# A four-layer decoder trunk: the retention gate's sample sum moved ahead of the norm's scale chain, and the first loads put in another order

## The reference

```python
def rmsnorm(x, g):
    x32 = x.astype(F32)
    return x32 * lax.rsqrt(jnp.mean(x32 * x32, axis=-1, keepdims=True) + EPS) * g

# even layer: one input projection, window attention [A] and spatial gating [B], SiLU gates, output projection
# odd layer (retention):
def odd_layer_prompt(x, g_mix, w_in, w_out):                 # the sample group: the same with a carried state
    q, k, v, g = split_ret(rmsnorm(x, g_mix) @ w_in, bsz, seq)   # 8 heads, keys 256 wide, values 512 wide
    state, o = lax.scan(step, state0, chunks(q, k, v))       # inner + cross per chunk of 128
    return ret_output(x, o, g, w_out), state

def ret_output(x, o, g, w_out):
    on = standardize(o).reshape(bsz, t, R_V_WIDTH)           # per head: (o - mean) * rsqrt(var + EPS)
    return x + (jax.nn.silu(g) * on) @ w_out

def memory_kv(mem, g_mem, w_k, w_v):                         # 256 memory tokens, once for each layer
    h = rmsnorm(mem, g_mem)
    return h @ w_k, h @ w_v
# every layer: cross attention into the memory (4 heads); at the end a last rmsnorm
```

## Time and profile before

| what | us |
|---|---|
| median of three runs | 3490.93 |
| the profiled execution's own time | 3490.97 |
| its span in the trace | 3489.2 |
| PE busy with matmuls | 3290.9 (94%) |
| GpSimd busy | 1052.2 (30%) |
| ACT busy | 998.0 (29%) |
| DVE busy | 916.1 (26%) |
| granted PE clock, mean of the span | 0.979 |

### The profile page before, as it was taken

How to read it: one execution, slowest core, us unless ns; L and a number is a source line. 1 busy time by engine, 2 the same in 40 slices (tenths; PEclk the granted TensorE clock), 3 DMA queues, 4 the chain that set the end, 5 groups by cost and what they waited for, 6 DMA issues and landing times.

```text
span 3489.2 us, 41826 instructions
## 1 busy us (share of the span) xinstructions
PE 3290.9 (94%) x15122; PEld 2567.9 (74%) x15122; DVE 916.1 (26%) x1684; ACT 998.0 (29%) x1526; POOL 1052.2 (30%) x444
## 2 busy tenths in 40 slices
PE   7999999999997999999999999999999989999976
PEld 5887777777886786776768677676867768878865
DVE  2202343332033413222130322214132240120335
ACT  5523333233233421312212131221212221222332
POOL 5632322332331232322313222231322223333311
PEclk9999999999999999999999999999999999999998
DMA  6432222223232243333333333333333344322332
GB/s 241 142 85 89 62 68 61 73 66 119 79 103 81 96 148 121 119 103 102 110 116 118 118 117 100 104 110 121 114 119 106 125 140 140 119 92 79 103 98 84
DMA packets 211053, 374.22 MB, mean 107 GB/s; under 512 B 20449, under 2 KB 59329, under 8 KB 207617
## 3 DMA queue, kind: packets, MB, share of 16 engines
q1 hardware_dynamic: 137744, 233.34, 21.5%
q10 hardware_dynamic: 73152, 138.60, 11.8%
HBM read 312.71 MB, written 60.16 MB: 107 GB/s over the span
## 4 chain that ended last, share of the span: by engine, by line
PE 75%; DVE 5%; ACT 2%; issue 1%; DVEq 1%; DMA 1%; ACTq 0%
PE bank L606 18%; PE bank L608 17%; PE bank L607 17%; PE bank L610 5%; PE bank L611 4%; PE bank L622 3%; PE bank L1032 2%; PE bank L1023 2%; PE bank L1071 1%; PE bank L1067 1%; PE bank L1063 1%; DVE R L1994 1%; DVEq L1782 1%; DVE R L2235 1%; PE bank L928 1%
## 5 line engine op out<-in xcount | busy, mean ns | idle before, releaser
L583 POOL TENSOR_TENSOR w_lo<-w_raw,w_hi 128x1024 fp32r<-128x1024 f32 x440 | 1052.0, 2391 | 2391.7 <-ACT w_hi L1138 2391.2
L606 PE MATMUL bank<-w_hi,xT_hi 128*128 128x512 f32 (+1 forms) x2880 | 1172.9, 407 | 6.5 <-ACT R L1150 2.7
L608 PE MATMUL bank<-w_hi,xT_lo 128*128 128x512 f32 (+1 forms) x2880 | 1125.2, 391 | 0.0
L607 PE MATMUL bank<-w_lo,xT_hi 128*128 128x512 f32 (+1 forms) x2880 | 1123.5, 390 | 0.0
L1138 ACT ACTIVATE w_hi<-w_raw 128x1024 fp32r<-128x1024 f32 x440 | 466.2, 1059 | 1537.6 <-PE bank L611 1437.8
L606 PEld LDWEIGHTS bank<-w_hi,xT_hi 128*128 128x128 f32 x2880 | 546.2, 190 | 144.3 <-issue 34.1
L608 PEld LDWEIGHTS bank<-w_hi,xT_lo 128*128 128x128 f32 x2880 | 544.6, 189 | 116.2
L607 PEld LDWEIGHTS bank<-w_lo,xT_hi 128*128 128x128 f32 x2880 | 546.0, 190 | 114.1 <-issue 11.5
L610 PE MATMUL bank<-w_hi,xT_sample 128*128 128x512 f32 (+1 forms) x816 | 333.4, 409 | 59.8 <-DVE R L1868 59.1
L611 PE MATMUL bank<-w_lo,xT_sample 128*128 128x512 f32 (+1 forms) x816 | 320.8, 394 | 0.0
L622 PE MATMUL bank<-cst,R 128*128 128x128 f32 (+3 forms) x1274 | 192.9, 277 | 61.5 <-DMA R<-in_norm_mem 13.5
(11 more groups left out here) (180 smaller groups left out, 2095.2 us busy)
## 6 DMA issues: line engine op xcount, KB each, us to landing
w_raw<-in_w_in_ret SPq DMA_DIRECT2D x128, 512.0 KB, 3.7
w_raw<-in_w_in_even SPq DMA_DIRECT2D x80, 512.0 KB, 3.6
w_raw<-in_w_in_ret SPq DMA_DIRECT2D x128, 256.0 KB, 2.9
R<-in_state_ret ACTq DMA_DIRECT2D x64, 512.0 KB, 4.4
out_ret_state_sample<-R ACTq DMA_DIRECT2D x64, 512.0 KB, 3.0
w_raw<-in_w_out_ret SPq DMA_DIRECT2D x64, 512.0 KB, 3.7
w_raw<-in_w_out_even SPq DMA_DIRECT2D x32, 512.0 KB, 3.7
mix_scratch<-R ACTq DMA_DIRECT2D x16, 576.0 KB, 3.4
```

What stands on the lines that cost most here:

```text
L583: pool.tensor_tensor(wlo[:, s], raw[:, s], whi[:, s].bitcast(F32), ALU.subtract).then_inc(lo_ready, 1)
L606: pe.matmul(acc, th[:, k, tok], hi[:, kk, 0:width], start=first, stop=False)
L607: pe.matmul(acc, th[:, k, tok], lo[:, kk, 0:width], start=False, stop=False)
L608: mm = pe.matmul(acc, tl[:, k, tok], hi[:, kk, 0:width], start=False, stop=last)
```

## The change

Two edits. In every retention head, DVE now does the gate's `sample_sum` right behind the variances (new function `group_vars`) and ahead of the wait for the root; it waits there for the end of product C (`w_used`). `gate_mul` is called with no counter for it and leaves the sum out. In the even layer `gate_mul` is as before.

At the start, the factors of the memory's two norms come in one load ahead of the memory tokens, the other four rows in two loads behind them, transposed apart at the end of the first product. The x loads move to the third group of the first product. ACT does `hi` of one weight group before it copies the factors, and the other three one by one between the first three halves of the transposed memory tokens.

```diff
-GAINS = ["norm_mix0", "norm_mix1", "norm_cross0", "norm_cross1", "norm_mem0", "norm_mem1"]
+GAINS = ["norm_mem0", "norm_mem1", "norm_mix0", "norm_mix1", "norm_cross0", "norm_cross1"]
+GM = 2 * KT
+GX = 4 * KT
...
-            tp(bank_of("mem", "gains")[:, 0:KT * len(GAINS)], grow[0:KT * len(GAINS), :], KT * len(GAINS)).then_inc(FULL("mem", "gains"), 1)
+            tp(bank_of("mem", "gains")[:, 0:GM], grow, GM).then_inc(FULL("mem", "gains"), 1)
...
+                elif ch == 0 and g == GPC - 1:
+                    pe.wait_ge(xgains_in, 32)
+                    pe.wait_ge(*is_free("mem", "xgains"))
+                    tp(bank_of("mem", "xgains")[:, 0:GX], xgrow, GX).then_inc(FULL("mem", "xgains"), 1)
...
             act.dma_start(cst[:, :], consts).then_inc(consts_in, 16)
+            act.dma_start(grow, I.norm_mem.rearrange("l (k p) -> (l k) p", p=P)).then_inc(gains_in, 16)
             for m in range(2):
                 act.dma_start(memX[:, m], I.mem_prompt[0, m * P:(m + 1) * P, :]).then_inc(mem_in, 16)
-            gains = [I.norm_mix[0], I.norm_mix[1], I.norm_cross[0], I.norm_cross[1], I.norm_mem[0], I.norm_mem[1]]
-            for n, g in enumerate(gains):
-                act.dma_start(grow[KT * n:KT * (n + 1), :], g.rearrange("(k p) -> k p", p=P)).then_inc(gains_in, 16)
-            load_x(False)
-            for s in range(RING):
-                hi(Lin(0), s)
+            for n, g in enumerate((I.norm_mix, I.norm_cross)):
+                act.dma_start(xgrow[GM * n:GM * (n + 1), :], g.rearrange("l (k p) -> (l k) p", p=P)).then_inc(xgains_in, 16)
+            hi(Lin(0), 0)
             act.wait_ge(*is_full("mem", "gains"))
...
             for n in range(3):
                 hi_half("mem", n, n, 0, "norm_mem0")
+                hi(Lin(0), n + 1)
...
+                    if g == 2:
+                        load_x(False)
...
-                v.wait_ge(w_used, L.at(GPC))
-                sample_sum(sbuf[0:NS, :], bank[NT], FREE(stage, (tag, NT)))
+                if L is not None:
+                    v.wait_ge(w_used, L.at(GPC))
+                    sample_sum(sbuf[0:NS, :], bank[NT], FREE(stage, (tag, NT)))
...
                 group_stats(NT)
+                group_vars(h)
+                v.wait_ge(w_used, Lin(L.c + GPC, L.k, L.i).at(GPC))
+                sample_sum(sgs[0:NS, :], bank[NT], FREE(stage, ("C", NT)))
                 group_norm(h)
-                gate_mul(stage, "C", i, 2 + h, Lin(L.c + GPC, L.k, L.i), lambda t: ON[0:rows(t), t], sg, sgs, NT)
+                gate_mul(stage, "C", i, 2 + h, None, lambda t: ON[0:rows(t), t], sg, sgs, NT)
```

More of the change, by code:

```diff
@@ L232, in make_plan @@
     weights("mem", 4)
-    plan.add("mem", [("gains", 5, True)])
+    plan.add("mem", [("gains", 5, True), ("xgains", 4, True)])
     state.xt = 1
@@ L369, in build @@
         gbc = c.take(D)
-        grow = gbc[:, 0:P]
+        grow, xgrow = gbc[0:GM, 0:P], gbc[0:GX, P:2 * P]
         junk = R2[:, 5 * D + 5 * CW:5 * D + 6 * CW]
@@ L432, in build @@
         rstd_ready, xt_hi_ready, stat_zero = sem("rstd_ready"), sem("xt_hi_ready"), sem("stat_zero")
-        gains_in, split_done = sem("gains_in"), sem("split_done")
+        gains_in, xgains_in, split_done = sem("gains_in"), sem("xgains_in"), sem("split_done")
         outs_done, x_saved = sem("outs_done"), sem("x_saved")
@@ L681, in _ @@
             pe.wait_ge(consts_in, 16)
-            pe.wait_ge(gains_in, 16 * len(GAINS))
+            pe.wait_ge(gains_in, 16)
             pe.wait_ge(*is_free("mem", "gains"))
-            tp(bank_of("mem", "gains")[:, 0:KT * len(GAINS)], grow[0:KT * len(GAINS), :], KT * len(GAINS)).then_inc(FULL("mem", "gains"), 1)
+            tp(bank_of("mem", "gains")[:, 0:GM], grow, GM).then_inc(FULL("mem", "gains"), 1)
             pe.wait_ge(mem_in, 32)
@@ L1248, in _ @@
             act.dma_start(cst[:, :], consts).then_inc(consts_in, 16)
+            act.dma_start(grow, I.norm_mem.rearrange("l (k p) -> (l k) p", p=P)).then_inc(gains_in, 16)
             for m in range(2):
                 act.dma_start(memX[:, m], I.mem_prompt[0, m * P:(m + 1) * P, :]).then_inc(mem_in, 16)
-            gains = [I.norm_mix[0], I.norm_mix[1], I.norm_cross[0], I.norm_cross[1], I.norm_mem[0], I.norm_mem[1]]
-            for n, g in enumerate(gains):
-                act.dma_start(grow[KT * n:KT * (n + 1), :], g.rearrange("(k p) -> k p", p=P)).then_inc(gains_in, 16)
-            load_x(False)
-            for s in range(RING):
-                hi(Lin(0), s)
+            for n, g in enumerate((I.norm_mix, I.norm_cross)):
+                act.dma_start(xgrow[GM * n:GM * (n + 1), :], g.rearrange("l (k p) -> (l k) p", p=P)).then_inc(xgains_in, 16)
+            hi(Lin(0), 0)
             act.wait_ge(*is_full("mem", "gains"))
-            copy(gT[:, :], bank_of("mem", "gains")[:, 0:KT * len(GAINS)]).then_inc(FREE("mem", "gains"), 1)
+            copy(gT[:, 0:GM], bank_of("mem", "gains")[:, 0:GM]).then_inc(FREE("mem", "gains"), 1)
             act.drain()
@@ L1292, in mem_his @@
                 elif ch == 1:
+                    if g == 0:
+                        act.wait_ge(*is_full("mem", "xgains"))
+                        copy(gT[:, GM:GM + GX], bank_of("mem", "xgains")[:, 0:GX]).then_inc(FREE("mem", "xgains"), 1)
+                        act.drain()
                     hi_half("mem", GPC + g, g, 256, "norm_mem1")
@@ L2222, in group_stats, with group_vars @@
                 do(v.bn_aggr(stat[0:r, 64 + 2 * c:66 + 2 * c], bn[0:r, 0:6]))
-            def group_norm(h):
+            def group_vars(h):
                 own, sam = bass.ds(h, 1), bass.ds(h + RH, 1)
@@ L2228, in group_norm @@
                 do(v.tensor_scalar(stat[0:NS, 55:56], stat[0:NS, 73:74], qd2[0:NS, sam], EPS, ALU.mult, ALU.add).then_inc(var_ready, 1))
+            def group_norm(h):
+                own, sam = bass.ds(h, 1), bass.ds(h + RH, 1)
                 v.wait_ge(std_ready, plan.st["gn"] + 1 + h)
```

## The result

The changed kernel takes 3438.24 us (median of 4 runs, 3435.19 to 3441.93), against 3491.35 us (4 runs, 3487.97 to 3492.68) of the kernel before beside it: a ratio of 0.985, 95% interval 0.9833 to 0.9867. That is 53 us gained where 76 were forecast. The sign and the place were right; the time lies 8 us above the top of the widest range (3430) and 17 us above the likeliest case (3421).

The account below looks back on a forecast made before the run. PE was taken to bound the kernel, with waits for `sample_sum` and at the start. Gains of 62.8 (seven heads), 5.1 (last head) and 8.3 (start), 76.2 us in all, took 3490.97 to 3414.8 us; range 3408 to 3430.

Parts of the forecast that it names:

- the widest range: Whole kernel: time from 3408 to 3430 us, with rival A and rival B included.
- the likeliest case: Whole kernel: time from 3409 to 3421 us around the forecast of 3414.8; the forecast itself had 71%.
- What bounds the kernel: Whole kernel: PE, busy 94% of the span; its longest waits were 59.1 us for `sample_sum` and 13.5 us at the start.
- the sum in the heads: Seven heads: `sample_sum` moved into DVE's wait for the root frees PE's sample tile earlier, 62.8 us gained in all.
- the term of 8.97 us a head: Each of seven heads: 7.13 us of PE's stall plus 1.84 us lost to the low clock, all gained.
- I count nothing for it here: Heads: one GpSimd subtraction blocking DVE puts the first two gated tiles at 1623.9, ahead of 1624.2; priced at nothing.
- the margin of 2.8: Heads: us between the first two gated tiles being ready (1621.43) and PE's transposes M00 asking for them (1624.2).
- rival A: Seven heads: GpSimd blocks normalization and gate products, 4.8 us; PE waits 2.0 us at M00, 14 us given back, 3429 us; 14%.
- The last head: Last head: M00 6.1 us earlier, less 1.0 us of clock; 5.1 us gained, bounds 4.2 and 6.1.
- the second stall: Last head: PE waits about 4.5 us at M00 for the second gated tile, which can lower the clock again.
- The start: Start: first product at 15.05, 9.4 us earlier, less 1.0 for blocks and 0.1 for a transpose; 8.3 us gained.
- rival B: Start: x takes the DMA engines from the weights; if nothing is hidden, 8.3 us are given back, 3423 us; 12%.
- a ring of four slots hides about that much: Start, within rival B: four weight slots cover about the 6 to 8 us by which two weight groups come late.

Follow-up runs that it names:

- the spaced loads: The changed kernel with x's five tiles asked for one by one, two groups apart: 3425.91 us, 12.3 us below the changed kernel.
- the hold: The changed kernel with ACT waiting, before it casts the next weights, until the second prompt tile is gated, in all eight heads: 3425.84 us.
- the kernel with both edits: The changed kernel with x's tiles asked for two groups apart and ACT's wait in all eight heads: 3414.74 us, 3417.2 us when run again.

## Why the prediction was wrong

**What bounds the kernel, and the sum in the heads: right.** The wait for `sample_sum` went in all seven heads, the sum hid in DVE's wait for the root, ACT's SiLU and bank 4 were early, and the slow clock of the earlier trace rows went too: behind a wait of 1.0 us M00's transposes took 0.66 us, about their normal 0.60. With GpSimd out of the way the period was 195.45 us, so the term of 8.97 us a head stands.

**The first failed step is "I count nothing for it here".** The prediction saw two subtractions coming, at 1617.8 to 1622.6, and put them beside the gate products alone. Its own rows don't say that: the normalization lasts from 1616.76 to 1619.80, so the first subtraction falls on it. The place was right (1612.68 in the changed kernel, whose product C ends some 5.0 us earlier there, is about 1617.7 on the old scale); what it lay beside was misread. Slowed by the first, the normalization was still under way at the second. The two cost it 6.88 - 3.04 = 3.84 us, beyond the margin of 2.8: a wait of 1.0 us in each head, 7 x 1.12 = 7.8 us. This is rival A's mechanism in a smaller form (both blocks on the normalization and none on the gate products, 3.84 us and not the 4.8 priced). The reason given against it, that 0.61 us a tile doesn't read as an instruction at double rate, was no evidence: the same line took 6.88, 4.89 and 3.04 us with two, one and no subtraction beside it. The Trainium skill's rule (SBUF — State Buffer, "Who interferes with whom") has the block for an instruction in a two-port mode too, and counts `tensor_scalar` among those that can be in one. These rows agree with it if the normalization is in such a mode, which no row shows directly. With the rule read so, the forecast would have been rival A's, 3429 us.

**The last head: mis-sized.** Forecast 5.1 us with bounds 4.2 and 6.1, measured 0.2. The term priced the second stall at 4.5 us and 1.0 us of clock, and forgot GpSimd altogether: two more blocks (2.39 - 0.23 = 2.2 us on L2247 and 4.89 - 3.04 = 1.9 us on L2251) made it 8.4 us, and the clock took 1.9. There is no margin in this head, so here each block counts in full. Without them the wait was 4.4 us, as forecast, and about 3 us more were gained.

**The start: rival B, at more than its price.** The first product came at 16.12 where 15.05 was forecast: the second token tile was in at 13.0, not at 12.1, and that is the one us missing there. Of the other 9.6, 8.7 went at the second product (it was to start at 52.92 - 8.3 = 44.6, and started at 54.38), and the rest behind it, where the clock was low. The failed step is that "a ring of four slots hides about that much". Rival B was given 12% and at the worst the start's 8.3 us; it took 10.6. Two things were missing in it. The first is the share: the rate was taken from the memory tokens, 3.3 us a megabyte, and applied evenly, while with rows of 8 KB in x's queue a group of weights took up to 19.0 us. The second is the order on ACT: the root stood behind two casts that waited, so the evacuation was late by the sum of both, 11.8 us; the ring can't hide this, since PE waits for a bank there and not for weights.

**Ledger of the two traces.** Start +2.3 (forecast -8.3), seven heads -55.2 (-62.8), the last head -0.2 (-5.1). Two pieces were in no term: -1.6 us ahead of the last sum, where the kernel before had a granted clock of 0.97 over its last 49 us and the changed one 1.00, and -1.1 in the rest of the program. Sum: -55.8 us. The gains of the two repairs are of the size of the losses at their places, by the medians: 12.3 us with the spaced loads (10.6 lost at the start), 12.4 with the hold (7.6 and 4.9 lost in the heads). The time with both is close to the forecast, 3414.7 and 3417.2 against 3414.8; it is the time of another kernel, and the forecast for this one stays wrong.

## What to carry to other kernels

When a stall goes, list what now runs beside what: the engines that used to work through the stall (here ACT's casts and GpSimd's subtractions) fall on another's chain, and a DVE step that starts beside a GpSimd step can last until that one ends, however short it is itself (0.16 us became 2.27). Where the chain has no slack, hold the feeder back for a few microseconds, with a wait that costs nothing elsewhere. And a transfer moved out of one stage's way is in the next stage's: ask for large loads piece by piece, and put nothing that others wait for behind a cast that waits for weights.

## What the runs showed of the hardware

- GpSimd's subtraction (2.4 us) stops DVE instructions of several kinds: TENSOR_SCALAR on 128x512 (3.04 to 4.89 and 6.88 us for five) and on 128x4 (0.23 to 2.39), SCALAR_TENSOR_TENSOR on 128x2 (0.16 to 2.27) and TENSOR_TENSOR on 64x512 (0.68 to 2.63, the row above). GpSimd is delayed as well: its two subtractions beside that product took 5.53 us, where two took 4.80 in the kernel before with DVE idle beside them (from 1626.58). A RECIPROCAL on 128x2 was not stopped: in the kernel with both edits it took 0.17 us at 37.75, in the second of two subtractions that ended at 39.43, while the TENSOR_TENSOR after it ended at 39.45:

```profile
37.75 0.17 DVE L1805 RECIPROCAL stat<-stat 128x2 f32<-128x2 f32 x1 [3.59 <-ACT stat L1241]
37.99 1.46 DVE L1806 TENSOR_TENSOR stat<-stat 128x2 f32<-128x2 f32 x1
```

```profile
34.68 4.75 POOL L585 TENSOR_TENSOR w_lo<-w_raw,w_hi 128x1024 fp32r<-128x1024 f32 x2 [0.54 <-ACT w_hi L1144]
```

- With both queues busy and the DMA engines full (394 and 410 GB/s over 5 us), the rows' size set how the queues shared them: with x in rows of 8 KB a weight group issued meanwhile took 9.6 to 19.0 us to land, with 2 KB 7.3 to 12.2. One trace with 2 KB stands behind this.
- The clock fell to 1.2 GHz behind the wait of 8.4 us (0.50 granted, above), and stayed at 2.4 GHz through the waits of 1.0 us in the seven heads: four M00 took 0.66 us behind them, 1.09 behind the long one.
